# Expert tiles from unscaled operands: the root applied to the sums, the scores between two tiles, and one wider view in v3

## The reference

```
xn   = rms_norm_2(x, norm2_g)                      # x * rsqrt(mean(x*x) + eps) * g
qh   = (xn @ peer_w_q)        -> [T, 8 heads, 2 halves, 128]
sub  = einsum("thpc,hpnc->thpn", qh, peer_sub_keys)        # 16 score vectors of 128 per token
v1, i1 = top_k(sub[:, :, 0], 16);  v2, i2 = top_k(sub[:, :, 1], 16)
vals, cidx = top_k(v1[..., :, None] + v2[..., None, :], 16)  # of 256 candidates
experts, gates = i1[...] * 128 + i2[...], softmax(vals)
y    = sum over the chosen experts of gelu(xn . u_e) * gate * v_e
```

## Time and profile before

| | us |
|---|---|
| median of 3 runs (3414.24 to 3420.36) | 3418.8 |
| the profiled execution's own time | 3417.98 |
| its span, first to last instruction | 3416.2 |
| PE busy in the span | 3254.5 (95%) |
| GpSimd busy | 2436.3 (71%) |
| VectorE busy | 1644.9 (48%) |
| ScalarE busy | 1485.3 (43%) |

### The profile page before, as it was taken

One profiled execution on the slowest core, in us unless ns is written; L12 is line 12 of the kernel. 1 busy time (PEld: TensorE's weight loads), 2 busy tenths in 40 slices (PEclk: granted clock), 3 DMA queues, 4 the chain that ended last, 5 costly groups with the idle time before them and its releaser, 6 DMA issues.

```text
span 3416.2 us, 64754 instructions
## 1 busy us (share of the span) xinstructions
PE 3254.5 (95%) x23654; PEld 2940.8 (86%) x23654; DVE 1644.9 (48%) x2960; ACT 1485.3 (43%) x1966; POOL 2436.3 (71%) x1048
## 2 busy tenths in 40 slices
PE   7899888999999999987898999999999999999999
PEld 5798788988888888886787999988888888888899
DVE  2047745622222222586763966677631774147600
ACT  3256543544444444433454553343354334433433
POOL 5630143888888888764386887777798778887787
PEclk9999999999999999998899999999999999999999
DMA  5843402565566555642254555545565555655455
GB/s 176 195 157 128 137 3 63 186 193 188 189 190 189 173 187 184 193 153 75 81 180 158 173 182 163 171 151 175 166 185 190 172 173 173 191 178 176 157 182 166
DMA packets 158085, 555.27 MB, mean 163 GB/s; under 512 B 17248, under 2 KB 23584, under 8 KB 157840
## 3 DMA queue, kind: packets, MB, share of 16 engines
q1 hardware_dynamic: 151008, 540.08, 50.1%
q0 software_dynamic: 2192, 8.20, 1.3%
q10 hardware_dynamic: 4768, 5.36, 0.5%
HBM read 548.33 MB, written 5.24 MB: 162 GB/s over the span
## 4 chain that ended last, share of the span: by engine, by line
PE 81%; issue 8%; POOL 6%; DVE 4%; ACT 1%; POOLq 0%; DVEq 0%; ACTq 0%
PE ps L615 34%; PE ps L606 23%; PE ps L617 17%; POOL wl L525 5%; PE ps L824 1%; PE ps L688 1%; PE ps L1062 1%; DVE uhl L1564 1%; PE ps L795 0%; DVE ehl L2130 0%; PE ps L697 0%; POOL xT L593 0%; PE ps L703 0%; DVE under_u L1538 0%; DVE arena L1640 0%
## 5 line engine op out<-in xcount | busy, mean ns | idle before, releaser
L525 POOL TENSOR_TENSOR wl<-raw,wh 128x1024 fp32r<-128x1024 f32 x984 | 2356.7, 2401 | 786.1 <-ACT wh L1147 785.6
L1147 ACT ACTIVATE wh<-raw 128x1024 fp32r<-128x1024 f32 (+1 forms) x1034 | 1086.2, 1053 | 1605.2 <-PE ps L617 1046.2
L615 PE MATMUL ps<-uhl,wh 128*128 128x512 f32 x3072 | 1079.1, 396 | 38.8 <-POOL wl L525 16.6
L606 PE MATMUL ps<-uhl,wh 128*128 128x256 f32 x4512 | 893.5, 289 | 26.9 <-ACT arena L1473 8.3
L617 PE MATMUL ps<-uhl,wl 128*128 128x256 f32 x3072 | 861.0, 280 | 0.0
L606 PEld LDWEIGHTS ps<-uhl,wh 128*128 128x128 f32 x4512 | 733.1, 195 | 35.4 <-issue 16.4
L615 PEld LDWEIGHTS ps<-uhl,wh 128*128 128x128 f32 x3072 | 579.7, 189 | 174.7 <-POOL wl L525 16.7
L606 PE MATMUL ps<-uhl,wl 128*128 128x256 f32 x2512 | 716.2, 285 | 0.0
L617 PEld LDWEIGHTS ps<-uhl,wl 128*128 128x128 f32 x3072 | 583.4, 190 | 0.1
L615 PE MATMUL ps<-ehl,wh 128*128 128x512 f32 x1536 | 553.0, 401 | 9.2 <-DVE ehl L2130 5.7
L606 PEld LDWEIGHTS ps<-uhl,wl 128*128 128x128 f32 x2512 | 488.3, 194 | 0.0
(11 more groups left out here) (340 smaller groups left out, 3008.9 us busy)
## 6 DMA issues: line engine op xcount, KB each, us to landing
raw<-w_u SPq DMA_DIRECT2D x256, 512.0 KB, 3.5
raw<-w_v SPq DMA_DIRECT2D x256, 512.0 KB, 3.5
raw<-w_gu SPq DMA_DIRECT2D x176, 512.0 KB, 3.5
raw<-w_down SPq DMA_DIRECT2D x80, 512.0 KB, 3.5
raw<-w_out SPq DMA_DIRECT2D x64, 512.0 KB, 3.5
raw<-w_z SPq DMA_DIRECT2D x54, 512.0 KB, 4.4
raw<-w_in SPq DMA_DIRECT2D x52, 512.0 KB, 3.5
raw<-w_qkv SPq DMA_DIRECT2D x48, 512.0 KB, 3.6
```

The source lines that it names most:

```text
L525: pool.tensor_tensor(wl[:, slot, 0:width], raw[:, slot, 0:width], wh[:, slot, 0:width].bitcast(F32), ALU.subtract).then_inc(lo_ready, 1)
L606: ins = pe.matmul(out, w[:, slot, at], x(c), start=first and c == n == 0, stop=last and c == kt - 1 and n == 2)
L615: pe.matmul(bank(b).rearrange("p (n t) -> p n t", n=2), wh[:, slot, at], pair[:, :, k0 + c, :], start=first and c == 0, stop=False, skip_g ...
L1147: act.activation(wh[:, slot, 0:width], raw[:, slot, 0:width], ACT.Copy).then_inc(hi_ready, 1)
```

## The change

Three edits, and one of size:

1. The root on the sums. `scale("n2b", 1)` and `round_u(1)` go. u0 to u3 read `UHL` as the queries do. The root goes to `rstdE`, at another place in the arena. Each expert tile's sums are multiplied by it on VectorE before gelu: in u0 by `scale_expert`, 28 of them at fixed places in the routing (after every second `top16`, every second block of candidates, and certain blocks of picks) and the last four behind the softmax; in u1 in `gate(..., tile=True)`; in u2 and u3 in `add_scale`. ScalarE's gelu waits for `exp_sum`.
2. The scores. PE computes the sub-key scores in four groups of eight after u0's tile 0, and ScalarE copies them before the first gelu.
3. v3 with `pair_unit`: the view `last_pair` covers both parts by one access pattern over a span of the memory, and VectorE adds two halves per tile.
4. The buffer of the parameters is rounded up to a multiple of eight words.

```diff
+PAR_WIDTH = -(-NPAR // 8) * 8
+SUB_BANKS = (4, 5, 6, 7, 2, 3, 4, 5)
...
+        SPAN = 2 * DT * T + 3 * RING * SLOT + PAR_WIDTH + KEEP + 2560 + QJ * T
+        with sb("span", SPAN + QJ * T, F32R) as span_:
...
+        rstdE = arena[:, 3 * QJ * T:3 * QJ * T + T]
...
+            def last_pair(c):
+                row = span_[:, c * T:(c + 1) * T]
+                return bass.AP(tensor=row.tensor, offset=row.offset, ap=[row.ap[0], [SPAN, 2], [1, T]])
...
-            pe.wait_ge(wq_ev, DT)
             pe.wait_ge(s_keys, 16)
-            for t in range(2):
-                for n in range(2 * PH):
-                    ins = pe.matmul(bank(4 * (1 - t) + n // 4)[:, (n % 4) * P:(n % 4 + 1) * P],
-                                    HQ[:, n, t * P:(t + 1) * P], KEYS[:, n * NK:(n + 1) * NK], start=True, stop=True)
-                ins.then_inc(sub_ps, 1)
+            pe.wait_ge(wq_ev, DT - 1)
+            def sub_scores():
+
+                pe.wait_ge(wq_ev, DT)
+                for k in range(4):
+                    if k == 3:
+                        pe.wait_ge(sub_ev, 2)
+                    for n in range(8):
+                        ins = pe.matmul(bank(SUB_BANKS[2 * k + n // 4])[:, (n % 4) * P:(n % 4 + 1) * P],
+                                        HQ[:, k % 2 * 8 + n, k // 2 * P:(k // 2 + 1) * P],
+                                        KEYS[:, (k % 2 * 8 + n) * NK:(k % 2 * 8 + n + 1) * NK], start=True, stop=True)
+                    ins.then_inc(sub_ps, 1)
...
                         pe.wait_ge(*((u_ev, i * 4 + (QJ * q + j - 1)) if q < 2 else
-                                     (exp_sum, i * 4 + (QJ * (q - 2) + j - 1))))
+                                     (exp_sum, i * 4 + (QJ * q + j - 1))))
...
+                        if first and q == 0 and j == 1 and n == 0:
+                            sub_scores()
...
-                            else:
-                                ins = unit(bank(d)[:, 0:T], i * 8 + (g + 1), g % RING,
-                                           lambda c: e_hi(q, UKT * s + c).rearrange("p a t -> p (a t)"),
-                                           lambda c: EL[q][:, UKT * s + c, :], first=s == 0, last=s == V_U - 1)
+                            ins = pair_unit(d, i * 8 + (g + 1), g % RING, EHL_PAIR[q] if q < NQ - 1 else None, UKT * s,
+                                            first=s == 0, last=s == V_U - 1)
...
-            pe.wait_ge(sub_ev, 8)
-            pe.wait_ge(u_ready, 5 * DT)
...
-            root(5, rstd, nrm)
+            root(5, rstdE, nrm)
...
-            round_u(1)
...
                     ahead(g, i, 8)
-                    if q < 2:
-                        act.wait_ge(w_used, i * 8 + (g + 2))
-                    else:
-                        act.wait_ge(exp_sum, i * 4 + (QJ * (q - 2) + j + 1))
+                    if first and j == 0:
+                        for k in range(4):
+                            sub_out(k)
+                    act.wait_ge(exp_sum, i * 4 + (QJ * q + j + 1))
...
-            scale("n2b", 1)
+            def scale_expert():
+
+                n = scaled[0]
+                scaled[0] += 1
+                dve.wait_ge(w_used, BASE["u0"] + 2 * n + 2)
+                dve.tensor_tensor(bank(n % 2)[:, 0:T], bank(n % 2)[:, 0:T], rstdE, ALU.mult).then_inc(exp_sum, 1)
+
+            scale_expert()
...
                     top16(SUB[:, t, n, :], top[:, t, n, :], topi[:, t, n, :].bitcast(U32), wk[:, n % 2, 0:NK])
+                    if n % 2:
+                        scale_expert()
...
                     top16(c, val[:, t, h, :], vali[:, t, 0, h, :].bitcast(U32), wk[:, h % 2, :])
+                    if h % 2:
+                        scale_expert()
...
                         link(dve.tensor_reduce(exs[:, t, n, h * TOPK:(h + 1) * TOPK], p1, AX, ALU.add))
+                    if h == 3 and t == 0 or t and h in (1, 4):
+                        scale_expert()
...
+            while scaled[0] < QJ:
+                scale_expert()
             dve.wait_ge(et_ps, 1)
...
+            def add_scale(b, i, done):
+
+                out = bank(4 + b)[:, 0:T]
+                add_halves(out, b % 2).then_inc(sums_scaled, 1)
+                dve.wait_ge(sums_scaled, i * 4 + done)
+                dve.tensor_tensor(out, out, rstdE, ALU.mult).then_inc(exp_sum, 1)
...
+                if tile:
+                    dve.wait_ge(w_used, i * 8 + (BASE["u1"] + 2 * m + 2))
+                    dve.tensor_tensor(bank(m % 2)[:, 0:T], bank(m % 2)[:, 0:T], rstdE, ALU.mult).then_inc(exp_sum, 1)
                 dve.wait_ge(g_ps, i * 4 + (GROUPS_Q * q + m + 1))
...
-                    if q < NQ - 1:
-                        dve.tensor_tensor(x, x, ps[:, d:d + 1, T:2 * T], ALU.add).then_inc(res_low, 1)
-                        dve.wait_ge(res_low, i * 2 + ((2 + q) * DT + d + 1))
+                    dve.tensor_tensor(x, x, ps[:, d:d + 1, T:2 * T], ALU.add).then_inc(res_low, 1)
+                    dve.wait_ge(res_low, i * 2 + ((2 + q) * DT + d + 1))
```

More of the change, by code:

```diff
@@ L225, in build @@
             pass
+        SPAN = 2 * DT * T + 3 * RING * SLOT + PAR_WIDTH + KEEP + 2560 + QJ * T
+        with sb("span", SPAN + QJ * T, F32R) as span_:
+            pass
         uhl_ = ctx.enter_context(sb("uhl", 2 * DT * T, F32R))
@@ L385, in build @@
         EH = EHL[:, 0]
-        EL = [EHL[:, 2 - q % 2] for q in range(NQ)]
+        rstdE = arena[:, 3 * QJ * T:3 * QJ * T + T]
+        EL = [EHL[:, 2 - q % 2] for q in range(NQ - 1)]
+        EL.append(view(span_[:, SPAN:SPAN + QJ * T], 0, QJ, T))
+        EH_LAST = view(span_, 0, QJ, T)
         EHL_PAIR = [EHL[:, 0:3 - q % 2:2 - q % 2] for q in range(NQ)]
@@ L392, in e_hi @@
                 return EH[:, j:j + n, :]
-            return uh[:, j:j + n, :] if j < DT else ul[:, j - DT:j - DT + n, :]
+            return EH_LAST[:, j:j + n, :]
         C0, Q0 = BASE["in2"], BASE["in2"] + 4 * EARLY
@@ L614, in pair_unit @@
                     at = slice(c * P, (c + 1) * P)
-                    pe.matmul(bank(b).rearrange("p (n t) -> p n t", n=2), wh[:, slot, at], pair[:, :, k0 + c, :],
+                    both = last_pair(k0 + c) if pair is None else pair[:, :, k0 + c, :]
+                    pe.matmul(bank(b).rearrange("p (n t) -> p n t", n=2), wh[:, slot, at], both,
                               start=first and c == 0, stop=False, skip_group_check=True)
-                    ins = pe.matmul(bank(b)[:, 0:T], wl[:, slot, at], pair[:, 0, k0 + c, :], start=False,
+                    ins = pe.matmul(bank(b)[:, 0:T], wl[:, slot, at], both[:, 0, :], start=False,
                                     stop=last and c == kt - 1, skip_group_check=True)
@@ L1468, in _, with sub_out @@
                     ahead(g, i, 4)
-            round_u(1)
[L1470 to L1474, removed]
+            def sub_out(k):
+                act.wait_ge(sub_ps, k + 1)
+                for n in range(2):
+                    at = k % 2 * 8 + 4 * n
+                    act.activation(SUB[:, k // 2, at:at + 4, :],
+                                   bank(SUB_BANKS[2 * k + n]).rearrange("p (n k) -> p n k", n=4), ACT.Copy)\
                         .then_inc(sub_ev, 1)
@@ L1478, in u_bank, with gelus @@
                 return j % 2 if q < 2 else 4 + j
-            def gelus(q, i, round_turn=None):
+            def gelus(q, i, round_turn=None, first=False):
                 for j in range(4):
@@ L1498, in round_experts @@
                 act.activation(e_hi(q, 4 * k, 4), HB[q][:, 4 * k:4 * k + 4, :], ACT.Copy).then_inc(eh_ready, 1)
-            with act.Fori(0, 7) as i:
+            gelus(0, 0, first=True)
+            with act.Fori(1, 7) as i:
                 gelus(0, i)
@@ L2042, in _ @@
                     dve.wait_ge(sums_scaled, i * 2 + (2 * FT + j + 1))
[L2043 removed]
+                    dve.tensor_tensor(HQ[:, bass.ds(i * 2 + j, 1), :].rearrange("p a t -> p (a t)"), sums, rstdE,
                                       ALU.mult).then_inc(wq_ev, 1)
[L2045 removed]
+            scaled = [0]
+            def scale_expert():
[4 more added lines that the diff above has]
+            scale_expert()
             def top16(values, best, index, work):
@@ L2112, in one_hots, with gate @@
                     .then_inc(oh_ready, 1)
-            def gate(q, i, m, last):
+            def gate(q, i, m, last, tile=False):
                 if m < 3 or not last:
                     one_hots(q, i, m + 1)
+                if tile:
+                    dve.wait_ge(w_used, i * 8 + (BASE["u1"] + 2 * m + 2))
+                    dve.tensor_tensor(bank(m % 2)[:, 0:T], bank(m % 2)[:, 0:T], rstdE, ALU.mult).then_inc(exp_sum, 1)
                 dve.wait_ge(g_ps, i * 4 + (GROUPS_Q * q + m + 1))
@@ L2145, in _ @@
                 for m in range(4):
-                    gate(0, i, m, False)
+                    gate(0, i, m, False, tile=True)
             for m in range(4):
-                gate(0, 7, m, True)
+                gate(0, 7, m, True, tile=True)
             for k in range(8):
```

10 lines of the change are left out of this document (3 added, 7 removed).

## The result

The changed kernel takes **3442.1 us** (median of 4 runs, 3433.8 to 3443.2) against 3419.6 for the kernel before (4 runs). The ratio is 1.0060, with a 95% interval from 1.0044 to 1.0077. It is slower, as forecast, and by more than the 14.7 us of the sum: 16 to 23 us by these three pairs of medians.

The account below looks back on a forecast made before the run. PE, busy 95% of the span, bounds the kernel, with other engines counting only where PE waits. From 3418.0 us, +18.3 (u0), +0.8, -4.9 and +0.5 gave 3432.7, forecast as 3433, range 3423 to 3441.

Parts of the forecast that it names:

- the sum: Whole kernel: all terms added, +18.3 + 0.8 - 4.9 + 0.5 = +14.7 us, giving 3432.7.
- The forecast case: u0: PE waits for late gelus before tiles 15, 16, 29 and 30 and nothing else; slower, chance 0.74.
- the range: Whole kernel: the measured time was expected between 3423 and 3441 us.
- The start of u0: u0 begins right behind the query matmuls; without further waits by PE it would end 11.9 us earlier.
- The queue on VectorE: u0: products at fixed places in VectorE's ordered queue delay gelu and PE; u0 ends 18.3 us later, early start included.
- The bullets: u0, tile by tile: late products cost PE 14.5 us by tile 16, 1.9 at tile 27, 9.3 before tile 30.
- tiles 1 to 8: u0: 3.4 us of routing work per 5.76 of PE, so VectorE waits for PE every time; no loss priced.
- Rival B: u0: the early lag is paid, but the last four tiles are scaled in time; 3421 us, chance 0.08.
- The clock: u0: 1.2 GHz follows the two long waits, before tiles 16 and 30; 2 x 2.3 us added.
- u1: u1: the product fits in VectorE's idle 2.0 us per tile and costs nothing; 14 us without that cover.
- u2 and u3: u2 and u3: the product shows only at each stage's end, +0.4 us each, +0.8 in all (0 to 1.4).
- v3: v3: 512-column matmuls bring 2.80 us per unit, -4.9 us; one more addition at the end, +0.5.

Follow-up runs that it names:

- e1: The changed kernel unedited, run a second time, against the kernel before: 3440.5 us, ratio 1.0051.
- e8: The changed kernel unedited, run a third time, against the kernel before: 3446.7 us, ratio 1.0078.
- e2: The changed kernel without u0's 32 products by the root, gelu waiting for PE alone: 3408.6 us, ratio 0.9963.
- e6: The changed kernel with two products in the first half's pick phase instead of one, three left for the end: 3443.2 us, ratio 1.0061.
- e4: The kernel before with only v3's wider view and the additions behind it: 3421.8 us, ratio 0.9989.

## Why the prediction was right, and where it was not

**Direction and case.** The forecast case came true: late gelus at four places of u0, nothing else on PE there. The median of 3442.1 lies just past the range's upper end of 3441, that of e1 just within, that of e8 5.7 us past it.

**The start of u0.** -11.9 was right in kind and size. Tile 0 stands right behind the queries, the scores took 7.14 where 7.41 was taken, and e2's floor of 185.7 us is 7.1 + 31 x 5.76.

**The queue on VectorE.** +18.3 predicted, +18.0 measured, in e1 1.2 more. Over the floor of 185.7 the stage lost 30.3 us, where the sum had 25.7 of waits and 4.6 of clock. That the total came out so exactly is partly luck: it is made of 23.0 of waits and 7.3 of other losses, among them three stretches of low clock in place of two (and 13.8 + 4.6 is 18.4, not 18.3). Within the queue, too, two things were off and offset each other. Four candidate sums were held by 1.1 to 2.0 us, some 6.4 in total, where the blocks of the earlier trace rows contained 1.5; and each product took 0.34 of the queue and not 0.45, as the next instruction starts before it ends. The PE waits were 6.1, 6.6, 2.5 and 6.9 where 4.8, 9.7, 1.9 and 9.3 came out; the clock fell behind three of them and not two.

**How that loss was told.** The bullets price each late tile as a loss of its own. As arithmetic this gives the end of u0, because the queue was followed to its end. As an account of causes it is wrong: e6 took 2.5 us of lateness off tiles 15 to 17 and gained nothing, where by this count each of them is a gain. The cause stands in the bullet that was passed over, tiles 1 to 8, where VectorE "waits for PE every time and saves nothing up". Rival B, which left out the end's wait and kept the rest, could not have come about in that way.

**The clock.** The granted clock fell to the 1.2 GHz level behind waits over 6 us and stayed at 1.00 behind the one of 2.5 us, as said. What was not foreseen: after u2's end, where PE waited 2.3 us for the last gelu (1.8 before), the row of the changed kernel shows 0.71, where the kernel before has 1.00. It costs 1.5 us in v1 (196.8 us against 195.3). It isn't the change's doing: e4, with the code of the kernel before and a wait of 1.80 us there, has it too, and e8, the changed kernel once more, does not.

```profile
2665.50:2669.50 4.00, 3.85 (x16) 3.28 (x17) 4.00 (x6) 0.00 (x0) 1.44 (x1) 0.71 0.61 204
```

**u1.** Nothing, as predicted: u1 and v0 took 0.4 more.

**u2 and u3: the step that failed.** "It shows only at each stage's end ... +0.8." The waits for gelu at the two ends grew by 0.9, from 3.6 to 4.5 us, as said. But it doesn't show only there: PE also waited for the product itself (L2137), once in each quarter and some 29 us behind its start, 1.1 us in sum. And the kernel without these products is 7 to 11 us faster by the medians, and u2 to v2 is 5 us shorter in the mean of the traces. Most of that is PE's pair units at their slow pace in 15 of 18 quarters. The changed kernel took 759.3 to 762.0 us there in three traces and the kernel before 752.5 and 754.0, so the term is 5 to 10 us in place of 0.8. The rest of the product's time was taken as hidden because PE isn't idle there, and but for those 1.1 us PE never was: its pace was another instead. What part of this the product causes, beyond the 1.3 to 2.0 us of waits, stays open.

**v3.** -4.9 + 0.5 predicted, -4.83 measured, and 4.8 less in e4 too.

**Sum.** 18.0 - 4.8 + 0.4 and 5 to 10 for u2 and u3 are 19 to 24 us, and the medians say 16 to 23.

## What to carry to other kernels

Where a small instruction is put into a strictly ordered queue that has other work to finish by a date, count the time that the queue will wait at that place, not only what it takes: here 32 products of 0.43 us cost 32 us (e2), and the same 32, one for each tile's time and with the candidate sums kept from being held, cost 0.3. A wait on the bounding engine tells where a loss shows; to find what makes it, move the thing that is late and see whether the end moves. When an instruction's duration jumps between two values, lay its start beside the timelines of the other engines, before anything is tuned on its mean. And when two traces differ, first count what differs between traces of the same code.

## What the runs showed of the hardware

**VectorE and GpSimd hold each other.** A sum of 128x256 with both operands in SBUF took 0.42 us, or up to 2.51 when it began within a split of GpSimd (2.40 us), and ended within 0.3 us of the split's end. With one operand in PSUM it took 0.41 to 0.42 sixteen times out of sixteen, though fifteen of these began within a split. The Trainium skill, page "GPSIMD Engine Reference", section "1. Specifications", says that GpSimd's SBUF interface is shared with VectorE and contended by VectorE's instructions with two SBUF inputs or in a 2-port performance mode. The traces agree for two inputs. Copies and casts with a single SBUF input were held too, as this one of the changed kernel, 0.39 when free and here within a split that ended at 2080.32; in what mode it ran no trace shows.

```profile
2078.11 2.45 DVE L2127 CAST misc<-misc 128x256 bf16<-128x256 f32 x1
```

**A stream of 512-column matmuls has more than one pace at full clock.** In every trace the pitch of a pair unit kept one value through most of a stage, and it was 2.77, 2.79, 2.80 or 2.83 us from stage to stage and from execution to execution, in stages that no edit touched as well (a stage of 96 units between 1142 and 1398 us, the code's `down`: 2.83 before, 2.79 after). The `down` stage, from its first conversion to the next stage's, took 255.0 us in the trace before and 250.4 in the trace after, which is 4.6 of the 5.7 us by which the pair differs ahead of every edit. Units of 256-column matmuls in u0 were at 2.88 in all traces. What chooses the pace stays open.

**A short wait is followed by a low clock in one execution and not in the next.** Behind PE's waits of 1.8 to 2.6 us at the start of u2, v1, u3 and v2 the granted clock was 0.50 for 3.4 us in 17 of 56 cases (14 traces), with the same waits and the same code on either side. Each cost 1.5 us.
